# Two fp32 blocks on one core: the low halves of the hyena projections' weight panels, subtracted on another engine

## What is computed

```python
def hyena_mixer(h, w_in, conv_w, conv_b, ..., skip, w_out):
    p = h @ w_in                                   # 1024 -> 4096
    u = short_conv(p[..., :3 * 1024], conv_w, conv_b)   # width 3, depthwise
    gate = p[..., 3 * 1024:]
    parts = jnp.split(u, 3, axis=-1)
    k_f = hyena_filters(L, ...)
    z = parts[0]
    for o in range(2):
        z = parts[o + 1] * long_conv(z, k_f[:, o], skip[o])
    return (z * jax.nn.silu(gate)) @ w_out
```

## Time and profile before

| what | value |
|---|---|
| median of 3 runs | 2055.29 us (2054.63 to 2056.0) |
| profiled execution, its own time | 2069.22 us |
| span of the trace | 2067.4 us |
| PE, DVE, ACT, POOL busy | 98%, 68%, 39%, 41% of the span |
| mean granted clock of TensorE | 0.984 of full speed |
| `split_lo` on GpSimd (L1844), all panels | 224, mean 2525 ns |

### The profile page before, as it was taken

One profiled execution on the slowest core, in us unless ns is written; L12 is line 12 of the kernel. 1 busy time (PEld: TensorE's weight loads), 2 busy tenths in 40 slices (PEclk: granted clock), 3 DMA queues, 4 the chain that ended last, 5 costly groups with the idle time before them and its releaser, 6 DMA issues.

```text
span 2067.4 us, 27071 instructions
## 1 busy us (share of the span) xinstructions
PE 2019.5 (98%) x10548; PEld 1585.7 (77%) x10548; DVE 1402.2 (68%) x2149; ACT 799.6 (39%) x1167; POOL 845.8 (41%) x550
## 2 busy tenths in 40 slices
PE   8989999999999999999999999999999999999998
PEld 7978788888878877788888887676877645767786
DVE  8772499995757268678897227437554776399964
ACT  3533333333234268433333223346664332322222
POOL 5824456654545431244444442234434213312232
PEclk9999999999999999999999999999999889999999
DMA  5032344443335341134434333113003213222221
GB/s 198 6 63 83 115 136 145 144 135 113 125 119 135 112 93 24 44 122 151 144 133 130 113 99 112 44 70 83 7 1 102 83 62 143 82 112 82 112 81 62
DMA packets 55615, 202.62 MB, mean 98 GB/s; under 512 B 7513, under 2 KB 8729, under 8 KB 52159
## 3 DMA queue, kind: packets, MB, share of 16 engines
q1 hardware_dynamic: 41552, 158.56, 23.6%
q0 software_dynamic: 13936, 42.34, 6.6%
HBM read 179.37 MB, written 10.49 MB: 92 GB/s over the span
## 4 chain that ended last, share of the span: by engine, by line
PE 85%; DVE 8%; ACT 3%; issue 2%; POOL 1%; DMA 0%; DVEq 0%; ACTq 0%; POOLq 0%
PE psum L740 16%; PE psum L745 16%; PE psum L741 16%; PE psum L790 3%; PE psum L791 3%; PE psum L792 3%; PE psum L1070 2%; PE psum L1048 2%; PE psum L630 2%; PE psum L1038 2%; PE psum L1117 2%; PE psum L1192 1%; POOL w_lo L1844 1%; PE psum L941 1%; PE psum L874 1%
## 5 line engine op out<-in xcount | busy, mean ns | idle before, releaser
L1844 POOL TENSOR_TENSOR w_lo<-raw,w_hi 128x1024 fp32r<-128x1024 f32 (+1 forms) x224 | 565.5, 2525 | 779.3 <-ACT w_hi L1325 779.2
L1325 ACT ACTIVATE w_hi<-raw 128x1024 fp32r<-128x1024 f32 (+1 forms) x224 | 233.8, 1045 | 843.7 <-PE psum L745 649.6
L740 PE MATMUL psum<-h_hi,w_hi 128*128 128x512 f32 x800 | 318.9, 399 | 1.5 <-ACT h_hi L1431 1.0
L741 PE MATMUL psum<-h_hi,w_lo 128*128 128x512 f32 x800 | 311.8, 390 | 0.0
L745 PE MATMUL psum<-h_lo,w_hi 128*128 128x512 f32 x800 | 197.9, 389 | 0.0
L740 PE MATMUL psum<-f_lo,w_hi 128*128 128x512 f32 x480 | 189.6, 395 | 1.7 <-POOL w_lo L1844 1.7
L741 PE MATMUL psum<-f_lo,w_lo 128*128 128x512 f32 x480 | 187.2, 390 | 0.0
L740 PEld LDWEIGHTS psum<-h_hi,w_hi 128*128 128x128 f32 x800 | 150.3, 188 | 38.6 <-ACT h_hi L1431 3.2
L741 PEld LDWEIGHTS psum<-h_hi,w_lo 128*128 128x128 f32 x800 | 150.3, 188 | 32.1 <-issue 2.2
L745 PEld LDWEIGHTS psum<-h_lo,w_hi 128*128 128x128 f32 x800 | 150.1, 188 | 31.3
L790 PE MATMUL psum<-f_hi,w_hi 128*128 128x512 f32 x352 | 138.3, 393 | 0.5
(11 more groups left out here) (508 smaller groups left out, 4133.8 us busy)
## 6 DMA issues: line engine op xcount, KB each, us to landing
raw<-in_ffn_w_up SPq DMA_DIRECT2D x88, 512.0 KB, 3.6
raw<-in_ffn_w_down SPq DMA_DIRECT2D x32, 512.0 KB, 3.5
raw<-in_hy_in SPq DMA_DIRECT2D x32, 512.0 KB, 5.7
ffn_buf<-in_ada_w POOLq DMA_DIRECT2D x28, 512.0 KB, 5.0
sq<-in_ada_w POOLq DMA_DIRECT2D x20, 512.0 KB, 5.0
raw<-in_ssm_w_glu SPq DMA_DIRECT2D x16, 512.0 KB, 3.6
spec<-big SPq DMA_DIRECT2D x8, 1024.0 KB, 3.8
big<-spec SPq DMA_DIRECT2D x8, 1024.0 KB, 4.8
```

The lines of the kernel that those rows point to most:

```text
L740: pe.matmul(o, hi[:, k, :], h_of(k), start=k == 0, stop=False)
L741: pe.matmul(o, lo[:, k, :], h_of(k), start=False, stop=False)
L1325: act.activation(w_parts(n)[0], raw[:, (n % 4) * HALF:(n % 4) * HALF + w], ACT.Copy).then_inc(S["w_hi"], 1)
L1844: pool.tensor_tensor(lo, raw[:, (n % 4) * HALF:(n % 4) * HALF + w], hi.bitcast(F32), ALU.subtract) \
```

## The change

DVE subtracts panels 2 to 31 of the hyena input projection. In turn n it makes panel n + 2: after the short convolution for n below 24, ahead of the gate for n from 24 to 29. The operation, its operands and its increment of w_lo are those of `split_lo`. DVE waits for w_hi as GpSimd did, and also for w_lo to have counted the panel before. GpSimd keeps panels 0 and 1 and does nothing more until it takes the eight panels of the output projection, for which it now waits first until w_lo has reached "wo3".

```diff
--- before.py
+++ after.py
@@ -1985,7 +1985,8 @@
                     i.then_inc(S["abs_used"], 1)
                 pool.wait_ge(S["abs_used"], 4 * u + 4)
                 pool.sem_inc(S["abs_sum"], 1)
-            for n in range(HALVES_AT["hy"] + 2, HALVES_AT["end"]):
+            pool.wait_ge(S["w_lo"], HALVES_AT["wo3"])
+            for n in range(HALVES_AT["wo3"], HALVES_AT["end"]):
                 split_lo(n)
 
 
@@ -2852,6 +2853,13 @@
                 TT(H_PARTS["wo3"][1][k], Z0[:, k, :], H_PARTS["wo3"][0][k].bitcast(F32), ALU.subtract) \
                     .then_inc(S["z_lo"], 1)
 
+            def z_panel(n):
+
+                dve.wait_ge(S["w_hi"], n + 1)
+                dve.wait_ge(S["w_lo"], n)
+                w, (hi, lo) = half_width[n], w_parts(n)
+                TT(lo, raw[:, (n % 4) * HALF:(n % 4) * HALF + w], hi.bitcast(F32), ALU.subtract).then_inc(S["w_lo"], 1)
+
             for n in range(32):
                 w, t = n // 8, n % 8
                 if w < 3:
@@ -2864,7 +2872,10 @@
                     frees(STT(g[:, 0:L - 1], z[:, 1:L], col("hyw", 48 + n), g[:, 0:L - 1], ALU.mult, ALU.add), key)
                     if n == 1:
                         filter_norm(3)
+                    z_panel(HALVES_AT["hy"] + n + 2)
                 else:
+                    if n < 30:
+                        z_panel(HALVES_AT["hy"] + n + 2)
                     dve.wait_ge(*free(("zg", t)))
                     dve.wait_ge(S["z_ready"], 8 + t + 1)
                     TT(Z0[:, t, :], Z0[:, t, :], SILU_G[t % 2], ALU.mult).then_inc(S["gate2"], 1)
```

## The result

The changed kernel took 2067.07 us (median of 4 runs, 2066.13 to 2068.82) against 2055.64 us (4 runs) before: 1.0053 times, 95% interval 1.0031 to 1.0075, so between 6 and 15 us slower. Timed twice more beside other kernels it took 1.0047 (1.0033 to 1.0060) and 1.0045 (1.0033 to 1.0057) times: some 9.5 us. The forecast was +7.95 us, and 2063.2 us as the time. The ratios on record are not those of the medians, and single long executions bear on them: two of the kernel before (2069.27 and 2072.47 us), one of e1 (2069.9), three of e2 (2074.1 to 2074.5), two of e4 (2076.5 and 2078.3) and two of e8 (2080.4 and 2080.9) took some 14 to 19 us more than the median of the same kernel.

What follows compares the result with a forecast made beforehand. It took PE, busy 98% of the span, as the bound. Stall 6.9 plus clock 1.75 less returned lockouts 0.7 gave +7.95 us, so 2063.2 us, range 2059.5 to 2068.0.

Steps and rivals of the forecast that it cites:

- 6.7 - 2: Lower bound of the total: a stall of 6.7 less a larger lockout return of 2, no clock cost; about +4.5 us.
- Part 2, the stall: PE at tile 26: panel 26, queued behind DVE's last spectrum, ready at 1972.9 against 1966.0 wanted; +6.9 us.
- Part 3, the clock: PE behind the stall at tile 26: lowered granted clock costs +1.75 us, bounds 0 to 3.4.
- Part 1, the lockouts returned: DVE before the first back transform: 3.0 us of lockouts returned, 2.3 us added by panels 12 and 13; net -0.7 us.
- Part 4: Elsewhere: GpSimd's removed subtractions and new wait, later raw buffer reloads and the gate tiles cost nothing.
- My slack of 0.75 us: Ordinary tiles: DVE has the panel ready at 1768.6, 0.75 us before its tile needs it; no cost.
- that the lockouts' return carries it: Rival, before tile 13: DVE freed of lockouts runs ahead, PE's waits and clock loss go, 5.5 us faster, 2049.8; chance 0.05.
- that the stall is absorbed: Rival, PE after tile 26: hidden slack takes up the stall, about 2055.3 + 0 to 3 us; chance 0.07.
- that the panel costs DVE 2.4 us: Rival, all DVE panels: 2.40 us each as on GpSimd, making tiles late, near 2083 us; chance 0.05.
- The profiled execution's surplus: Whole kernel: median lies 13.9 us below the profiled 2069.22 us; the difference was carried over from 2077.2 to 2063.2.

Runs made afterwards that it cites:

- e1: Changed kernel with panel 26 alone back on GpSimd, the other 29 on DVE; 2055.46 us, 1.0017 times the kernel before.
- e2: Changed kernel with panel 26 one place earlier in DVE's queue, between products and sums of spectrum 7; 2056.08 us, 1.0039 times the kernel before.
- e4: Changed kernel with 14 useless filler matmuls on PE ahead of tile 26; 2062.73 us, 1.0057 times the kernel before.
- e8: Changed kernel with the same 14 filler matmuls, timed once more; 2064.47 us, 1.0063 times the kernel before.
- e0: Changed kernel again, nothing altered, as the measure for other runs; 2063.36 us, 1.0047 times the kernel before.
- e7: Changed kernel once more, nothing altered, beside the kernel with filler matmuls; 2063.50 us, 1.0045 times the kernel before.
- e3: Kernel before with only panel 26 moved to DVE, at the place the change gives it; 2061.94 us, 1.0033 times the kernel before.
- e6: Changed kernel with two more useless 128x1024 DVE operations right ahead of panel 26; 2071.06 us in one run.
- e5: Kernel before with GpSimd delaying panels 13 and 14 until spectra 0 and 1 are summed, nothing on DVE; 2048.88 us, 0.9977 times the kernel before.

## Why the prediction was right

The size came out at the upper end: 2067.07 us lies 3.9 above the forecast and 0.9 below the upper bound of 2068.0, and by the medians the change cost 11.4 us, 10.5 (e0) and 9.9 (e7) where 7.95 were forecast. The ruler gives 9.7 in the stage; what the first timing has beyond that is not located. In the range's working 6.7 - 2 is 4.7 and not 4.5, and the bounds come to 2059.8 and 2067.8 instead of 2059.5 and 2068.0; nothing hangs on it.

**Part 2, the stall.** Forecast 6.9 us from a chain added up of rows; measured 6.86. Its chain, from the convolution of tile 23 to the end of panel 26, was added up to 15.75 us and is 15.74 (1944.50 to 1960.24). Its terms held one by one: panel 1.22 us (I took 1.21), lockouts gone, panel 24 and 25 in time for their tiles. e1 and e2 take away the stall and leave 29 or all 30 panels on DVE, e3 brings it with one panel, e6 stretches it by what is put in front.

**Part 3, the clock.** Forecast +1.75, bounds 0 to 3.4. It was the term that was mis-sized: 3.0 us by the granted clock of the changed kernel's trace, 2.2 in e0 and e7. The nearest row was a wait of 3 us with a granted clock of 0.57 for 4 us behind it; behind 6.9 us it was 0.62 for 8 us.

**Part 1, the lockouts returned.** Forecast -0.7. DVE's chain up to the release of PE's bank did shorten by that: from 1807.47 to 1838.83 before it is 31.36 us, and from 1795.67 to 1826.30 after it is 30.63. PE began the back transform earlier by just that, 16.15 us after the start of panel 14 instead of 16.87. Its wait there still grew from 3.12 to 3.64 us, since PE came to it 1.25 us earlier: its two waits of 0.3 us and the slower matmuls behind them were gone. From panel 14 to 16 only 0.39 is left (34.91 to 34.52), and in the five traces with about 36.4 us nothing. I had written that panel 14 stands behind the step that releases the bank, and so costs nothing. It stands in front of the fold that releases the next bank, where PE has a new wait of 0.4 us on L2778. On the other hand 0.4 us came back before another back transform (16.35 to 15.93), where I had looked for nothing: the twenty records of that back transform took 4.48 us instead of 4.88. DVE's row of 3.37 us, 10 us ahead of it, is 1.22 after the change; that this is the reason is not shown by a run of its own.

**What was missed.** Part 4 said that no other tile is late. Tile 2 is: PE waits 0.65 us for panel 2. DVE comes to it late from the filters' spectra, where it stands 4.04 us behind a store:

```profile
1730.11 0.69 DVE L2753 TENSOR_TENSOR big<-big,psum 128x512 f32<-128x512 f32 x1 [4.04 <-DMA spec<-big]
...
1734.36 1.22 DVE L2861 TENSOR_TENSOR w_lo<-raw,w_hi 128x1024 fp32r<-128x1024 f32 x1
```

My slack of 0.75 us was that of an ordinary tile; the first panel has a queue of its own in front. It costs 0.77 us from panel 3 to 4.

Summed by the ruler: 9.76 at tiles 26 and 27 and 0.77 at tile 2, less 0.39 and 0.42, is 9.7, against 7.95 forecast. **The rivals**: that the lockouts' return carries it fell with PE's wait before the first back transform, 3.6 us where 3.1 stood; e5 shows what the return is worth without the load, 4.2 us of the 5.5 that I had given it; that the stall is absorbed fell with the ruler, 29 to 33 is 21.76 us in both; that the panel costs DVE 2.4 us fell with the 1.22. **The profiled execution's surplus** of 13.9 us over the median, which I carried over as if it belonged to profiling, was the clock in the stretch from 1635 us. It did no harm, since only a difference was forecast; the changed kernel's profiled execution took 2066.53 us, 0.5 below its median.

## What to carry to other kernels

An engine's share of busy time doesn't say whether it can take more work; lay the rows of its queue end to end up to the new operation and compare with the moment at which it is wanted. Thirty operations moved: one at the wrong place cost nearly 10 us, two others (panels 2 and 14) less than 1 us each, and the rest no wait of PE. When two engines lock each other out, try first to delay the one that has slack until the other works on operands that don't collide; here that gained 4 us where moving the work lost 10.

## What was not expected of the hardware

The half clock behind a wait is not fixed by the wait: behind 3.6 us before the same back transform the tiles took 34.5 us in some executions and 36.4 in others. The same sixteen records of it, in the changed kernel and in e0:

```profile
1828.69 4.32 PE L1192 MATMUL psum<-big 128*128 128x256 f32 x16 [0.38 <-DVE rms L2778]
```
```profile
1824.90 6.21 PE L1192 MATMUL psum<-big 128*128 128x256 f32 x16 [0.79 <-DVE rms L2778]
```

PE had started again at 1826.36 us in the one and at 1822.57 in the other, and in both the granted clock was 1.00 only from 1830 us on: 3.6 and 7.4 us behind the wait. Behind 1.80 us (e5) PE ran at nearly its full pace, 4.92 us for twenty records against 4.53.

The lockout goes both ways: in e1 GpSimd's one subtraction beside a dense DVE took 3.44 us instead of 2.40, and the DVE operation that starts 1.1 us after it took 3.41 instead of 1.22.

```profile
1947.94 3.44 POOL L1844 TENSOR_TENSOR w_lo<-raw,w_hi 128x1024 fp32r<-128x1024 f32 x1 [246.60 <-ACT w_hi L1325]
```
```profile
1949.05 3.41 DVE L2806 TENSOR_TENSOR scr<-scr,big 128x1024 f32<-128x1024 f32 x1
```
